# A two-block transformer step on one core: the mixer's input projections ahead of its gates, the state space scan in chunks of eight steps, the gates between the steps of the recurrence

## The chip, the cores and the metric

The kernel is one program on one core of a Trainium2 chip. TensorE (PE) multiplies, VectorE (DVE) and ScalarE (ACT) do the elementwise work, GpSimd (POOL) and SyncE (SP) issue the transfers; they meet only at semaphores. The metric is the device time of one execution in microseconds (us), less is better.

## The reference, cut to what matters

The input is one sequence of 512 tokens of 1024 values. The first block projects it once and mixes four branches of 256 values; each branch is weighted by a sigmoid gate of its own, and the sum goes through `w_o`. A feed forward net and a second block (two attention layers) follow, which the change leaves alone.

```python
mod = (c_act @ ada_w[l] + ada_b[l])[:, None, :]          # 6 x 1024 values: shifts, scales, gates
sh1, sc1, gt1, sh2, sc2, gt2 = jnp.split(mod, 6, axis=-1)
h = rms_norm(x, norm_mix_g[l]) * (1.0 + sc1) + sh1
p = h @ w_in[l]
y_a, v_first = rwkv7_mixer(p[..., :OFF_B], ...)          # a recurrence over 4 heads of 64 x 64
y_b = spatial_gating_mixer(p[..., OFF_B:OFF_C], ...)
y_c = short_conv_mixer(p[..., OFF_C:OFF_D], ...)
y_d = s5_mixer(p[..., OFF_D:OFF_G], ...)                 # 16 groups of 16 channels, 64 complex states each
gates = jax.nn.sigmoid(p[..., OFF_G:]).reshape(bsz, seq, N_BRANCH, D_MODEL)
merged = (gates[:, :, 0] * y_a + gates[:, :, 1] * y_b
          + gates[:, :, 2] * y_c + gates[:, :, 3] * y_d)
x = x + gt1 * (merged @ w_o[l])
h = rms_norm(x, norm_ffn_g[l]) * (1.0 + sc2) + sh2
x = x + gt2 * (jnp.square(jax.nn.relu(h @ ffn_w1[l])) @ ffn_w2[l])

# s5_mixer: x_t = a x_(t-1) + B u_t (complex, diagonal a), y = Re(C x) + d u
_, _, x_re, x_im = lax.associative_scan(_complex_affine_combine, (ar, ai, bu_re, bu_im), axis=1)
y = (jnp.einsum('gcn,bsgn->bsgc', c_re, x_re) - jnp.einsum('gcn,bsgn->bsgc', c_im, x_im))
h = jax.nn.gelu(y) @ glu_w
return h[..., :D_MODEL] * jax.nn.sigmoid(h[..., D_MODEL:])
```

## The kernel before, in words

**Pieces and tiles.** Activations lie transposed, 128 channels on the partitions and 512 tokens along a row. All large weights come as one stream of pieces of 128x1024 (512 KB) in the order in which PE uses them, into a ring of four slots. GpSimd fetches each piece twice: as it is (`load_high`, L330), and, after it has written its negative (L335), added to that (`load_low`, L338), which leaves the rounding rest. So every product of fp32 values is three fast matmuls (high by high, high by rest, rest by high; L1290), and a piece is 24 matmuls over 512 tokens. `project(n, owner)` multiplies n pieces by the eight tiles of `h`, one output tile of a PSUM bank for a piece; `branch_out` multiplies a piece by the two tiles of a branch's result, four output tiles for a piece. There are four such banks (`ps[0]` to `ps[3]`): a product waits until the tile four before it was read by its `owner`. The other four banks (`PA` to `PD`) serve everything else. Every engine runs its own list in program order; `need(name)` waits for the next count of a semaphore. `tile()` waits for the next finished tile, `skip(n)` passes over n tiles that another engine reads.

**Start.** `modulate` (DVE, L448 and L450) multiplies each piece of `ada_w` (48 of them, 512 KB, eight for each of six groups of 1024 outputs) by a value of `c_act` and adds it up; `modulation(group)` on PE (L1314) then sums over the partitions with eight matmuls of one column, fp32, each recorded twice. Groups 0 and 1 are done before `norm` (L412, L414, L366, L367: scale, shift, high part, rest) writes `h`.

**Mixer.** PE takes 12 pieces for the convolution, the spatial gating and s5, does the small matmuls of the spatial gating, and then works through gates and branch outputs beside the s5 scan: `BESIDE` says how many gate pieces and which `branch_out` stand after each of its eight steps. On DVE the scan builds tables of cosines and sines over 512 steps (L887 to L897), then for each of eight tiles of states rotates, scans twice and rotates back (L904 to L920). Seven pieces for `rwkv` follow, s5's gates and outputs, the small matmuls that build the 32-step blocks of the recurrence (`blocks`, L1517), an inversion of triangular blocks on DVE (L555, L556) that is turned around through DRAM by eight transfers (L287), and the recurrence: 16 steps on PE (L1541 to L1560), each with four round trips to DVE and ACT (`rec_y`, `rec_sa`, `rec_state`, `state_set`). At its end stand the last gates, rwkv's output, the modulation's third group (eight more pieces through DVE), the merging of the branches (L841, L848, L366, L367), `w_o` with the fourth and fifth group beside it, the norm, and the feed forward net. The mixer and `w_o` take 61 + 8 pieces.

**ACT** computes the gates' sigmoids (`gate()`, L1091) into a place given by `gate_room(p)`; DVE's `gated(f)` multiplies a branch's tile by it.

Of the kernel before, what the change touches and what calls it, by code (L numbers as in the profile page):

```python
# [28 lines left out]
C = 32  # L29
# [8 lines left out]
S5T = 8  # L38

# [25 lines left out]
BESIDE = [(2, None), (2, 0), (2, None), (2, 1), (1, None), (1, None), (1, None), (1, 1)]  # L65
# [53 lines left out]
def build(nc, A, out):  # L119
# [6 lines left out]
    with ExitStack() as ctx:  # L126
# [24 lines left out]
        arena = sb("arena", [P, ARENA])  # L151
        eye_r = sb("eye_r", [P, P], F32R)
# [7 lines left out]
        t_dram = nc.dram_tensor("pair_inverse", (2, H_A, NCK, C // 2, C), F32, kind="Internal").ap()  # L160

# [26 lines left out]

        def gate_room(p):

            at = (ARENA - 4 * T, ARENA - 4 * T, ARENA - 5 * T, 2048 if p < 28 else 4096)[p // 8] + p % 4 * T
            return arena[:, at:at + T]

        merged, product, glu = x, work[:, 0, :], work[:, 1, :]
        ada_m = place([("sum", (2, D)), ("ada", (ADA, D))], at=ARENA - (ADA + 2) * D)
        conv_m = place([("bg", (2, T)), ("cg", (2, T)), ("z", (2, T)), ("y", (2, T))])
        sg_m = place([("z", (4, T)), ("mu", (T,)), ("d", (2, T)), ("sq", (2, T)), ("std", (T,)), ("rstd", (T,)),
                      ("vn", (2, T)), ("vt", (2, 4, P)), ("ws", (4, P)), ("wsm", (4, P)), ("bs", (2, P)),
                      ("mix", (2, T)), ("caus", (P,))], at=4096)
        s5_m = place([("ct", (8, T)), ("st", (8, T)), ("w", (6, T)), ("bt", (2, 8, P)), ("bpad", (2, 8, P)),  # L200
                      ("bb", (2, 8, 16)), ("b_in", (2, 8, 16)), ("m8", (8, 8)), ("c_in", (2, 2, P)), ("u", (2, T))])
        s5_m["cc"] = s5_m["bpad"]
        assert s5_m["end"] <= ARENA - 4 * T
# [9 lines left out]
                       at=max(rw_in["end"], rw_bd["end"]))  # L213
# [34 lines left out]
        def _(sp):  # L248
# [3 lines left out]
            for q in range(ADA):  # L252
                sp.dma_start(ada[:, q, :], A["ada"][q]).then_inc(S(f"ada_in{q}"), 16)
# [733 lines left out]
        def _(act):  # L987
# [114 lines left out]
            for k in range(4):  # L1102
                gate()
# [656 lines left out]
```

## Time and profile before

| | |
|---|---|
| runs | 2538.32, 2542.22, 2545.75 us, median 2542.22 |
| profiled execution | 2537.91 us, span of the core 2536.1 us |
| busy | PE 2212.2, DVE 1420.2, POOL 845.3, ACT 441.1 us |
| mean granted clock of PE | 0.922 |

The span is the time from the first to the last instruction. "Busy" is the time in which an engine had an instruction under way. The granted clock is the share of 2.4 GHz that PE's clock gate let through: 0.5 is 1.2 GHz, 1.0 is 2.4 GHz.

### The profile page before, as it was taken

The numbers are of one execution on the slowest core, as the hardware profiler recorded it, in microseconds if no ns is written. First come the engines' busy times: TensorE is split into PE (matmuls) and PEld (weight loads), VectorE is DVE, ScalarE is ACT, GpSimd is POOL, SyncE is SP. The second block draws the span as 40 slices with busy tenths as digits, with TensorE's granted clock in tenths as the row PEclk, the third lists the DMA queues.
The fourth block names the chain that finished last, engine by engine and source line by source line (L and its number), as shares of the span: only waits on it lengthen the run. The fifth ranks groups of instructions, "written<-read, shape, count | busy, mean of one in ns | idle before, by whom it ended". The sixth has DMA issues, their size and how long they took to land.

```text
span 2536.1 us, 26355 instructions
## 1 busy us (share of the span) xinstructions
PE 2212.2 (87%) x10172; PEld 1736.6 (68%) x10172; DVE 1420.2 (56%) x1964; ACT 441.1 (17%) x871; POOL 845.3 (33%) x1009
## 2 busy tenths in 40 slices
PE   1967999668787999999988999999898679999995
PEld 1745667557665888887854787878677338878784
DVE  6459775763567344256545572736563665727364
ACT  1010002101000000021056220201210562202021
POOL 1312333110232444444410444444433004444442
PEclk9978999875797999999987999999999789999998
DMA  7635667530695999998820898989877108989895
GB/s 252 135 65 108 141 136 164 96 80 1 174 298 152 205 193 196 191 193 179 183 61 1 193 193 181 195 177 196 194 163 174 31 1 187 193 179 194 182 194 125
DMA packets 115269, 390.31 MB, mean 154 GB/s; under 512 B 20516, under 2 KB 21412, under 8 KB 114632
## 3 DMA queue, kind: packets, MB, share of 16 engines
q0 software_dynamic: 96624, 350.46, 64.8%
q1 hardware_dynamic: 18520, 38.16, 4.3%
q8 instruction: 81, 1.33, 0.2%
q14 instruction: 44, 0.36, 0.0%
HBM read 385.88 MB, written 2.62 MB: 153 GB/s over the span
## 4 chain that ended last, share of the span: by engine, by line
PE 72%; DVE 17%; DMA 5%; ACT 3%; issue 2%; POOL 0%; SPq 0%; DVEq 0%; ACTq 0%
PE ps L1290 61%; DMA arena<-in_ada 3%; PE ps L1379 2%; PE ps L1360 2%; PE ps L1395 1%; DMA w_lo<-in_w 1%; DVE small L706 1%; DVE arena L450 1%; ACT arena L1231 1%; PE ps L1517 1%; ACT arena L1239 1%; DVE work L555 1%; DVE h_lo L367 1%; DVE arena L733 1%; PE ps L1476 1%
## 5 line engine op out<-in xcount | busy, mean ns | idle before, releaser
L1290 PE MATMUL ps<-h_hi,w_hi 128*128 128x512 f32 x1760 | 713.6, 405 | 39.0 <-DVE h_lo L367 27.9
L1290 PE MATMUL ps<-h_lo,w_hi 128*128 128x512 f32 x1760 | 695.7, 395 | 0.0
L1290 PE MATMUL ps<-h_hi,w_lo 128*128 128x512 f32 x1760 | 694.6, 395 | 0.0
L330 POOL DMA_DIRECT2D w_hi<-in_w x334 | 185.7, 556 | 1516.0 <-PE ps L1290 1515.2
L1290 PEld LDWEIGHTS ps<-h_hi,w_hi 128*128 128x128 f32 x1760 | 336.7, 191 | 132.6 <-DVE h_lo L367 28.3
L1290 PE MATMUL ps<-g_hi,w_hi 128*128 128x512 f32 (+1 forms) x880 | 345.6, 393 | 52.0 <-DVE g_lo L367 21.7
L1290 PEld LDWEIGHTS ps<-h_lo,w_hi 128*128 128x128 f32 x1760 | 337.2, 192 | 74.2 <-issue 6.9
L1290 PEld LDWEIGHTS ps<-h_hi,w_lo 128*128 128x128 f32 x1760 | 336.9, 191 | 71.8
L335 POOL TENSOR_SCALAR w_lo<-w_hi 128x1024 fp32r<-128x1024 f32 x334 | 358.6, 1074 | 35.9 <-DMA w_hi<-in_w 30.1
L1290 PE MATMUL ps<-g_lo,w_hi 128*128 128x512 f32 (+1 forms) x880 | 341.6, 388 | 0.0
L1290 PE MATMUL ps<-g_hi,w_lo 128*128 128x512 f32 (+1 forms) x880 | 341.1, 388 | 0.0
L338 POOL DMA_DIRECT2D w_lo<-in_w x334 | 300.4, 899 | 106.0 <-POOL w_lo L335 106.0
L1290 PEld LDWEIGHTS ps<-g_hi,w_hi 128*128 128x128 f32 x880 | 169.4, 192 | 97.0 <-DVE g_lo L367 24.3
L1290 PEld LDWEIGHTS ps<-g_hi,w_lo 128*128 128x128 f32 x880 | 169.6, 193 | 33.3
L1290 PEld LDWEIGHTS ps<-g_lo,w_hi 128*128 128x128 f32 x880 | 169.5, 193 | 32.6 <-issue 0.7
L1256 ACT ACTIVATE arena<-arena,vec 128x512 f32<-128x512 f32 x88 | 71.8, 816 | 412.2 <-DVE arena L728 404.7
L739 DVE TENSOR_TENSOR x<-ps,x 128x512 f32<-128x512 f32 x48 | 33.2, 692 | 183.9 <-PE ps L1290 183.9
L733 DVE SCALAR_TENSOR_TENSOR arena<-arena,vec 128x511 f32<-128x511 f32 x88 | 113.9, 1294 | 3.6 <-ACT arena L1256 0.6
L728 DVE TENSOR_TENSOR arena<-ps,work 128x512 f32<-128x512 f32 x88 | 60.9, 692 | 91.9 <-PE ps L1290 90.5
L960 DVE TENSOR_TENSOR arena<-arena 128x512 f32<-128x512 f32 x32 | 50.3, 1570 | 77.7 <-ACT arena L1178 77.7
L966 DVE SCALAR_TENSOR_TENSOR x<-ps,mod,x 128x512 f32<-128x512 f32 x32 | 24.0, 751 | 111.6 <-PE ps L1290 111.5
L366 DVE CAST g_hi<-arena 128x512 fp32r<-128x512 f32 (+1 forms) x100 | 80.6, 806 | 6.3 <-ACT arena L1112 2.9
(343 smaller groups left out, 2126.7 us busy)
## 6 DMA issues: line engine op xcount, KB each, us to landing
w_hi<-in_w POOLq DMA_DIRECT2D x334, 512.0 KB, 3.9
w_lo<-in_w POOLq DMA_DIRECT2D x334, 512.0 KB, 5.6
arena<-in_ada SPq DMA_DIRECT2D x48, 512.0 KB, 8.8
x<-in_xT SPq DMA_DIRECT2D x1, 2048.0 KB, 17.3
x<-in_xT SPq DMA_DIRECT2D x4, 512.0 KB, 4.7
arena<-in_memT SPq DMA_DIRECT2D x2, 1024.0 KB, 5.4
out_y<-arena SPq DMA_DIRECT2D x1, 2048.0 KB, 6.3
work<-in_mask_dil SPq DMA_DIRECT2D x1, 640.0 KB, 5.9
```

The costliest lines, as they stand in the source:

```text
L330: pool.dma_start(w_hi[:, q % SLOTS, :], A["w"][q]).then_inc(S(f"high_in{q % SLOTS}"), 16)
L335: pool.tensor_scalar(w_lo[:, q % SLOTS, :], w_hi[:, q % SLOTS, :].bitcast(F32), -1.0, 0.0, ALU.mult, ALU.add).then_inc(S("negated"), 1)
L338: pool.dma_start(w_lo[:, q % SLOTS, :], A["w"][q], accum_op=ALU.add).then_inc(S(f"low_in{q % SLOTS}"), 16)
L366: do(dve.tensor_copy(hi, src))
L728: do(dve.tensor_tensor(cv_m["z"][:, side, :], tile()[:], rstd, ALU.mult), "conv_scaled")
L733: do(dve.scalar_tensor_tensor(dst[:, 1:], z[:, :T - 1], w(1), dst[:, 1:], ALU.mult, ALU.add))
L739: update = lambda k: do(dve.tensor_tensor(x[:, k, :], tile()[:], x[:, k, :], ALU.add), "x_done")
L960: do(dve.tensor_tensor(s, r, r, ALU.mult), "relu_used")
L1256: do(act.activation(c[:, j % 2, :], cv_m["z"][:, side, :], ACT.Identity, scale=V("cw2", at), bias=V("cb2", 44 * layer + 22 * side + j0 + j ...
L1290: mm = pe.matmul(bank, w[:, slot, cols], a(k), start=(k == 0 and i == 0), stop=(k == blocks - 1 and i == 2))
L1360: mm = pe.matmul(bank(g)[:, 0:width], at_m["q"][half(g), pair, P * qb:P * qb + P], keys, start=True, stop=not fox)
L1379: mm = pe.matmul(ps[6 + pair % 2][64 * g:64 * g + 64, q0:T], values, pt[pair % 2][:, g, b, q0:T], start=(b == 0), stop=(b == blocks - 1))
```

## The change

The mixer is put into another order and two of its parts are computed in another way; what is computed stays.

- The modulation's groups 0, 1 and 2 leave DVE: `modulation_piece` multiplies each piece of `ada_w` on PE by a single column of `c_act` and adds in PSUM, eight fp32 matmuls of one column for a piece. `modulate` stays for groups 3 to 5. GpSimd's first fetch of weights waits for eight of these pieces.
- s5 works in chunks of Q = 8 steps: the outputs inside a chunk come from a Toeplitz matrix (`toep`), the chunks' states from one scan over 64 chunks for all eight tiles at once. Its tables (`f`, `g`, the kernels) are computed on DVE at the start and by 16 transposes and 32 small matmuls on PE; the kernels, the inputs `u` and the outputs `y` are turned around through DRAM by 8, 16 and 16 transfers.
- Order of the pieces: all 19 input projections first, with the small matmuls of the spatial gating between them, then gates and outputs. Four gate pieces stand between the `blocks`, eight beside the inversion, and 13 pieces are cut into 52 parts of six matmuls, of which three stand in each step of the recurrence (`beside`, `product_steps`). DVE and ACT take their share of that work (`gate_steps`, `step_beside`) in set turns.
- Both norms of the first block write the high part on ACT (`high_shifted`).
- The clearing of the recurrence's padded blocks goes from DVE to ACT (`clear`), between gates.

```diff
-    order = [("conv_in", 6), ("sg_in", 4), ("s5_in", 2)]
-    for branch in ("conv", "sg"):
-        order += [(branch + "_gate", 4), (branch + "_out", 1)] * 2
-    order += [("rwkv_in", 7)] + [("s5_gate", 4), ("s5_out", 2)] * 2
-    return order + [("rwkv_gate", 4), ("rwkv_gate", 4), ("rwkv_out", 1), ("rwkv_out", 1)]
+    order = [("conv_in", 6), ("sg_in", 4), ("s5_in", 2), ("rwkv_in", 7)]
+    order += [("conv_gate", 4), ("conv_out", 1)] * 2
+    order += [("sg_gate", 4), ("sg_out", 1), ("sg_gate", 4), ("s5_gate", 4), ("sg_out", 1)]
+    order += [("s5_gate", 1), ("s5_out", 1)] * 4
+    return order + [("rwkv_gate", 8), ("rwkv_out", 2)]
...
+            pool.wait_ge(S("ada_taken"), 8)
             for q in range(ahead):
                 load_high(q)
...
+            def modulation_piece(q, slots):
+                pe.wait_ge(S(f"ada_in{q % ADA}"), 16 * (q // ADA + 1))
+                for k in range(8):
+                    col = q // 8 * 8 + k
+                    mm = pe.matmul(PA[:, col:col + 1], slots[:, q % ADA, P * k:P * k + P], small[:, 0, q % 8:q % 8 + 1],
+                                   start=(q % 8 == 0 and k == 0), stop=(q % 8 == 7 and k == 7), skip_group_check=True)
+                mm.then_inc(S("ada_taken"), 1)
...
+            for q in range(12):
+                modulation_piece(q, ada_first)
+            pe.wait_ge(S("s5_f"), 1)
+            for i in range(4):
+                for s in range(4):
+                    mm = pe.transpose(ps[i][:, P * s:P * s + P], m["f"][:, i // 2, 4 * (i % 2) + s, :], K("ident"))
...
+            for q in range(12, 16):
+                modulation_piece(q, ada_first)
             total_squares(work[:, 2, :])
-            modulation(0)
-            modulation(1)
+            pe.wait_ge(S("s5_e"), 4)
             project(10, ["dve_freed"] * 6 + ["act_freed"] * 4, ready=h_tile)
...
+                for k in range(KT):
+                    do(dve.scalar_tensor_tensor(work[:, 4 + k % 2, :], x[:, k, :], gain(k), work[:, 3, :], ALU.mult, ALU.mult), "norm_scaled")
+                    if k:
+                        low(k - 1)
+                low(KT - 1)
...
+            for r in range(Q):
+                for k in range(2):
+                    sp.dma_start(s5_m["u_turned"][16 * r:16 * r + 16, 8 * k:8 * k + 8, :],
+                                 u_dram[:, :, k, Q - 1 - r, :].rearrange("g p n -> p g n")).then_inc(S("s5_u_in"), 16)
...
             blocks(pad("a"), pad("b"), 64, 8)
+            project(1, "gate")
             blocks(pad("k"), pad("a"), 64, 8)
+            project(1, "gate")
...
             blocks(pad("b"), lambda p, c: K("ident"), P, 4)
+            branch_out(1, 4)
             project(4, "gate")
+            project(4, "gate")
+            def beside():
+                y = lambda b: (lambda k: g_hi[:, 2 * b + k, :], lambda k: g_lo[:, 2 * b + k, :])
+                slot = open_piece()
+                for i in range(4):
+                    yield from product_steps(slot, 2, *y(1), "gated", first_block=2 * i, first=(i == 0))
+                for _ in range(4):
+                    yield from product_steps(open_piece(), 8, *h, "gate")
+                    slot = open_piece()
+                    for i in range(4):
+                        yield from product_steps(slot, 2, *y(2), "glu_gate" if i % 2 else "gated", first_block=2 * i, first=(i == 0))
+                for _ in range(4):
+                    yield from product_steps(open_piece(), 8, *h, "gate")
...
             for c in range(NCK):
...
+                next(steps, None)
                 if c:
                     need("rec_o_copied", 2)
                 for p in range(2):
                     need("rec_y_copied1" if p else "rec_y_copied")
                     pe.matmul(ps[6 + p][rows[p], 0:HD], bd["tT"][rows[p], c, :], chain_y[rows[p], 0, :],
                               start=True, stop=True).then_inc(S("rec_sa"), 1)
+                next(steps, None)
...
-            project(3, "gate")
+                next(steps, None)
+            for _ in steps:
+                pass
+            project(4, "gate")
             pe.wait_ge(S("o_padded"), 2)
...
-            project(1, "gate")
             pe.wait_ge(S("rw_out"), 2)
-            for half in range(2):
-                branch_out(3, 4)
-            modulation(2)
+            branch_out(3, 8)
+            for q in range(16, 24):
+                modulation_piece(q, ada_m["ada"])
             project(7, "x_done", ready=lambda k: need("merged"))
```

The instructions of PE at the start of the program, before; the names are tiles (`work`: the sum of squares, `arena`: the modulation's sums, `con`: a column of ones), and a row is a kind of instruction with its count.

```order
L1322 MATMUL ps<-work,con 128x512 [waits square_used,con_in]
L1314 MATMUL ps<-con,arena 128x1 [waits ada_sum]
L1314 MATMUL ps<-con,arena 128x1 x7
L1314 MATMUL ps<-con,arena 128x1 [waits ada_sum]
L1314 MATMUL ps<-con,arena 128x1 x7
L1290 MATMUL ps<-h_hi,w_hi 128x512 [waits h_ready,low_in0]
```

The same place of the changed kernel, from the twelfth piece of the modulation on:

```order
L1501 MATMUL ps<-small,arena 128x1 [waits ada_in3]
L1501 MATMUL ps<-small,arena 128x1 x7
L1597 MATMUL ps<-con,arena 128x128 [waits s5_f]
L1597 MATMUL ps<-con,arena 128x128 x15
L1602 MATMUL ps<-arena 128x16 x32
L1501 MATMUL ps<-small,arena 128x1 [waits ada_in0]
L1501 MATMUL ps<-small,arena 128x1 x7
...
L1509 MATMUL ps<-work,con 128x512 [waits square_used]
L1460 MATMUL ps<-h_hi,w_hi 128x512 [waits h_ready,low_in0,s5_e]
```

Where 16 matmuls of one column stood behind the sum of squares, 128 of them (16 pieces), 16 transposes and 32 small matmuls now stand ahead of it.

A step of the recurrence on PE before (`work` holds state and copies, `arena` the blocks):

```order
L1541 MATMUL ps<-arena 64x64 x2
L1545 MATMUL ps<-work,arena 64x64 [waits state_set] x2
L1550 MATMUL ps<-work,arena 64x64 [waits rec_y_copied,rec_o_copied]
L1550 MATMUL ps<-work,arena 64x64 [waits rec_y_copied1]
L1553 MATMUL ps<-arena 128x64 x2
L1556 MATMUL ps<-work,arena 128x64 [waits rec_sa_copied]
L1556 MATMUL ps<-work,arena 128x64 [waits rec_sa_copied1]
```

and in the changed kernel, at the start of its second step:

```order
L1759 MATMUL ps<-arena 64x64 [waits state_set]
L1760 MATMUL ps<-work,arena 64x64
L1759 MATMUL ps<-arena 64x64 [waits state_set]
L1760 MATMUL ps<-work,arena 64x64
L1460 MATMUL ps<-g_hi,w_hi 128x512 [waits gate]
...
L1460 MATMUL ps<-g_hi,w_lo 128x512
L1766 MATMUL ps<-work,arena 64x64 [waits rec_y_copied,rec_o_copied]
L1766 MATMUL ps<-work,arena 64x64 [waits rec_y_copied1]
L1460 MATMUL ps<-h_hi,w_hi 128x512 [waits gated,low_in3]
...
L1460 MATMUL ps<-h_hi,w_lo 128x512
L1770 MATMUL ps<-arena 128x64
```

Six matmuls of a branch output or a gate now stand between the two places at which PE waits for the copies of DVE and ACT, six more ahead of the state's update, and six behind the step.

## Rows read from the trace of the kernel before

**Rows 1.** Windows of the span: length, busy time and instructions by engine, granted clock, DMA.
```profile
core 0: us, PE busy (x) PEld busy (x) DVE busy (x) ACT busy (x) POOL busy (x), PEclk, DMA share, GB/s
0.00:60.20 60.20, 8.83 (x34) 7.65 (x34) 36.45 (x63) 11.90 (x18) 10.02 (x17) 1.00 0.78 266
...
140.20:365.00 224.80, 177.23 (x652) 127.12 (x652) 186.77 (x287) 20.14 (x30) 56.24 (x66) 0.85 0.48 102
365.00:489.70 124.70, 103.95 (x438) 81.97 (x436) 75.82 (x88) 24.93 (x36) 43.27 (x52) 0.92 0.71 150
489.70:557.10 67.40, 42.45 (x544) 37.92 (x544) 48.46 (x92) 3.68 (x5) 10.03 (x12) 0.83 0.44 87
557.10:633.00 75.90, 67.89 (x512) 53.95 (x512) 23.65 (x94) 13.50 (x62) 0.00 (x0) 0.50 0.00 1
633.00:793.60 160.60, 119.25 (x472) 91.60 (x471) 103.29 (x131) 12.64 (x19) 38.22 (x45) 0.78 0.70 203
```

**Rows 2.** Timeline, ACT reads a gate's tile: start, length, wait before it.
```profile
205.17 0.60 ACT L1091 ACTIVATE arena<-ps 128x512 f32<-128x512 f32 x1 [4.84 <-PE ps L1290]
```

**Rows 3.** Timeline of PE: the modulation's sums, at the start and in the feed forward net.
```profile
41.93 3.41 PE L1314 MATMUL ps<-con,arena 128*128 128x1 f32 x16
845.80 1.84 PE L1314 MATMUL ps<-con,arena 128*128 128x1 f32 x16
```

**Rows 4.** Timeline of PE: four transposes, loads for two matmuls, rwkv's last small matmuls.
```profile
153.91 1.11 PE L1421 MATMUL ps<-con,arena 128*128 128x128 f32 x4 [6.88 <-DVE arena L825]
558.82 0.50 PEld L1553 LDWEIGHTS ps<-arena 64*128 64x128 f32 x4
654.80 7.26 PE L1568 MATMUL ps<-con,arena 64*128 64x32 f32 x39
```

**Rows 5.** Two windows of the stretch in which L1568 runs, columns as in rows 1.
```profile
652.00:656.00 4.00, 4.00 (x38) 4.00 (x37) 0.00 (x0) 0.60 (x1) 0.00 (x0) 0.91 0.53 102
656.00:660.00 4.00, 4.00 (x22) 4.00 (x20) 2.50 (x4) 0.00 (x0) 0.00 (x0) 0.50 0.02 4
```

**Rows 6.** Timeline: the norms' last tiles, and the second one's chain from its sum on.
```profile
76.91 0.69 DVE L367 TENSOR_TENSOR h_lo<-work,h_hi 128x512 fp32r<-128x512 f32 x1
764.69 2.06 PE L1322 MATMUL ps<-work,con 128*128 128x512 f32 x2
772.30 0.75 DVE L412 SCALAR_TENSOR_TENSOR work<-x,small,work 128x512 f32<-128x512 f32 x1
792.92 0.69 DVE L367 TENSOR_TENSOR h_lo<-work,h_hi 128x512 fp32r<-128x512 f32 x1
```

**Rows 7.** Timeline of DVE: the s5 tables' first and eighth round, one tile's start, the next's.
```profile
179.13 0.17 DVE L887 TENSOR_TENSOR arena<-arena,small 128x8 f32<-128x8 f32 x1
205.57 1.23 DVE L887 TENSOR_TENSOR arena<-arena,small 128x1024 f32<-128x1024 f32 x1
234.30 0.69 DVE L904 TENSOR_TENSOR arena<-ps,arena 128x512 f32<-128x512 f32 x1
245.53 0.69 DVE L904 TENSOR_TENSOR arena<-ps,arena 128x512 f32<-128x512 f32 x1
```

**Rows 8.** Timeline: PE's blocks, DVE's inversion, its transfer through DRAM, the recurrence's first matmuls.
```profile
489.77 9.98 PE L1517 MATMUL ps<-arena 128*64 128x64 f32 x256 [18.52 <-DVE arena L521]
516.81 1.39 DVE L555 TENSOR_TENSOR work<-arena 128x32 f32<-128x32 f32 x1
549.53 0.34 SPq L280 DMA_DIRECT2D pair_inverse<-arena  x1
557.11 0.48 PE L1541 MATMUL ps<-arena 64*64 64x64 f32 x4 [19.34 <-DMA arena<-pair_inverse]
```

**Rows 9.** Timeline of DVE behind the recurrence: rwkv's output, merging's first and last operation.
```profile
662.17 0.69 DVE L596 TENSOR_TENSOR arena<-arena,ps 128x512 f32<-128x512 f32 x1 [3.42 <-PE ps L1568]
687.25 0.69 DVE L841 TENSOR_TENSOR work<-ps,arena 128x512 f32<-128x512 f32 x1
708.19 0.69 DVE L367 TENSOR_TENSOR h_lo<-x,h_hi 128x512 fp32r<-128x512 f32 x1
```

More of the change, by code:

```diff
@@ L548, in vector_recurrence @@
                 bd_copy(rw_bt, per=4)
+                skip(4)
+                for f in range(4):
+                    gated(f)
                 dve.wait_ge(S("a_in"), 16 * 9)
@@ L1100, in glu_gate, with clear @@
                 count[1] += 1
-            for k in range(4):
-                gate()
-            skip(4)
-            for gates, branch in BESIDE:
-                for k in range(gates):
-                    gate()
-                if branch is not None:
-                    skip(4)
-            for k in range(2):
-                need("s5_sum")
-                do(act.activation(m["w"][:, 2 + k, :], m["w"][:, k, :], ACT.Gelu_apprx_tanh), "s5_gelu")
+            def clear(i):
+                do(act.activation(rw_pad["all"][:, 2048 * i:2048 * i + 2048], K("ident")[:, 0:1].broadcast_to((P, 2048)), ACT.Copy, scale=0.0),
+                   "rw_cleared")
             v = rw_in
@@ L1292, in product @@
                             mm.then_inc(S("w_used"), 1)
+                    if k % 2 and k < blocks - 1:
+                        yield
                 mm.then_inc(S("tile"), 1)
@@ L1447, in _ @@
[L1447 to L1454 removed]
+                    for g in range(2):
+                        mm = pe.matmul(ps[4 + part][halves[g], NQ * s:NQ * s + NQ], m["e"][:, part, s, halves[g]], m["u_turned"][:, 2 * s + g, :],
+                                       start=True, stop=True)
@@ L1459, in branch_out @@
                     for i in range(4):
-                        product(slot, 2, *y, "glu_gate" if glu_tiles and i % 2 else "gated", first_block=2 * i, first=(i == 0))
-            inputs(0)
-            project(4, "gate")
+                        product(slot, 2, *y, "gated", first_block=2 * i, first=(i == 0))
+            v, bd = rw_in, rw_bd
+            project(2, "gate")
+            pe.wait_ge(S("lora_in"), 16)
+            pe.wait_ge(S("rw_m"), 2)
+            pe.wait_ge(S("s5_out"), 2)
@@ new lines, in adapted @@
+            def adapted(rows, first_bank, after=None):
+                for k in range(2):
+                    if after is not None:
+                        pe.wait_ge(S(after), k + 1)
+                    pe.matmul(ps[first_bank + k][:], lora[rows, P * k:P * k + P], v["m"][rows, :],
+                              start=True, stop=True).then_inc(S("rw_adapted"), 1)
+            adapted(slice(0, 32), 4)
+            adapted(slice(32, 64), 6)
+            project(2, "gate")
+            adapted(slice(64, 128), 4, "rw_decay")
@@ L1464, in _ @@
             pe.wait_ge(S("conv_y"), 2)
             branch_out(0, 4)
-            for s, (gates, branch) in enumerate(BESIDE):
-                project(gates, "gate")
-                if s < S5T - 1:
-                    need("s5_bu_used")
-                    inputs(s + 1)
-                if branch is not None:
-                    pe.wait_ge(S("sg_y" if branch else "conv_y"), 2)
-                    branch_out(branch, 4)
-                need("s5_states")
-                for part in range(2):
-                    mm = pe.matmul(ps[6 + s // 4][:], m["cc"][:, part, s, :], m["w"][:, 4 + part, :],
-                                   start=(s % 4 == 0 and part == 0), stop=(s % 4 == 3 and part == 1))
-                mm.then_inc(S("s5_read"), 1)
```

626 lines of the change are left out of this document (380 added, 246 removed).

## The prediction

> **What bounds the kernel now.** I read the windows first [rows 1]. From 140 to 490 us PE is busy for 281 of 349.5 us and DVE for 263: neither engine is full, they wait for each other in turns. From 489.7 to 557.1 PE builds blocks and then stands still until the inverted blocks come back through DRAM. From 557.1 to 633 the recurrence runs alone: 16 steps in 75.9 us, 4.74 each, at a granted clock of 0.50 and with DVE busy for a third of it. In the tail to 793.6 us PE works 119 of 160.6 us. Behind the second norm (its last tile ends at 793.6 [rows 6]) 1742.5 us follow that the change doesn't touch. So the sum has to find only where that last tile ends afterwards. The profiled execution took 2537.91 us (2536.1 of span and 1.8 outside it), 4.3 under the median of 2542.22; I sum in its own time and add 4.3 at the end.
>
> The unit of the sum is a piece of weights. Where only gates stand in line, ACT reads a tile every 0.60 + 4.84 = 5.44 us [rows 2]: 24 matmuls, 0.227 us each.
>
> **Start, to the last tile of the first norm (before: 77.6 us [rows 6]).** Sixteen pieces of modulation come off DVE and become 128 matmuls of one column, each recorded twice. The nearest row has the same form: 8 such matmuls take 3.41 us at the start, 1.84 after a long run of products [rows 3]. I take 3.41, since PE does nothing but such small work here. DMA brought 266 GB/s in these 60 us [rows 1], about 2 us for a piece of 512 KB, so PE and no longer DVE or DMA sets the pace. First piece done at about 7.5 us (my estimate), twelve more 40.9, 16 transposes 4.4 (1.11 for four), 32 small matmuls of two records at 0.125 are 7.8 [rows 4], the last three and the sum's own start counted as four pieces, 13.6: 74.2 us. Then the sum of squares and the root as in the second norm, 7.6 (764.69 to 772.30 [rows 6]): 81.8. The new norm leaves DVE two operations a tile, 16 of 0.75 with a little between them, 12.8 us, where the norm of before took 21.3 (772.30 to 793.61). Together 94.6, **17.0 us later** than before. The s5 tables, now at the start on DVE, are hidden by the 74 us of PE. With 1.84 a piece this stage would end 25 us sooner; that is the gain's bound. The Trainium skill ("TensorE: Matmul & The Clock Gate", section "What's actually happening") says that the throttled state is the default and activity releases it; by it sustained small matmuls might get 1.84. The row speaks against it: with PE busy for 4.00 of 4.00 us at L1568 the granted clock fell from 0.91 to 0.50 [rows 5].
>
> **To the first block (before 77.6 to 489.8, 412.2 us with 51 pieces).** Now 29 pieces stand there. 28 of them at 5.44 are 152.3, the first starts with 1.8 of its own. The small matmuls (the spatial gating, the transposes, the adapted inputs and the head sums of rwkv, s5's inputs 3.4 and its 48 outputs 8) I put at 25.8, by 0.125 to 0.28 us for a record or transpose [rows 4]. Waits at 26.3: 16.6 for the padded inputs of the blocks (18.52 before [rows 8], less the clearing that ACT takes), 4.9 where squares wait for DVE's tables, 2.5 at a root, 1.6 for s5's states, 0.7 for a cold start. What goes is the scan: its tables by doubling (from 179.1 to 205.6 and on) and eight tiles of 11.2 us each (234.30 to 245.53) [rows 7], which is why PE waited. Its replacement is one scan of 64 chunks for all tiles; the turns of `u` and `y` through DRAM lie beside the rwkv and gate pieces, with about 8.5 and 9 us to spare. Eight transfers with the first write took 7.6 us (549.53 to 557.11 [rows 8]), so sixteen take under 15.2 and fit. Sum 206.4: the blocks start at **301**. Of the 189 us, 22 x 5.44 = 120 are pieces only moved behind this point; 69 are waits gone, plus the loss of the start.
>
> **Blocks and inversion (before 489.8 to 557.1, 67.4 us).** The blocks' matmuls and waits were some 26.4 us (to 516.8 on DVE [rows 8]); four gates between them add 21.8, and 2.8 of clearing go: 45.4. DVE then inverts (516.81 to 549.53, 32.8 us) and the transfer takes 7.6, with 5.44 + 1.6 ahead of it for a piece and reads queued in front: 47.4. PE puts a branch output and eight gates beside that, nine pieces, 49.0. The two are about equal, so PE sets the end: with 1 to 2 us for late weights the recurrence starts at **396.5**.
>
> **Recurrence (before 75.9).** In each step stand 18 product matmuls, 18 x 0.227 = 4.08 us, and its 32 small records. Those took 67.9 of 75.9 us over 16 steps, 4.2 us a step, at clock 0.50 [rows 1]; the products hold the clock near 1, so I take half, 2.1, and 0.2 for changes between the forms. 6.4 us a step, 102.4 in all: it ends at **499**. The round trips to DVE and ACT (4.74 - 4.2 = 0.5 us of wait a step before) are covered by parts of six matmuls, 1.36 us, if DVE and ACT come to the copies in time. Uncovered, or with the small ones at 4.2, a step costs up to 8.5.
>
> **Tail (before 160.6).** With R the end of the recurrence: four parts 5.4 and four gates 21.8 with 1.4 between, the last small matmuls of rwkv 10 (L1568: 7.26 for 39 records [rows 4]): R + 38.6. rwkv's output and the merge: the latter took 21.6 us (687.25 to 708.88) behind the modulation's third group, which held DVE for most of the time from 662 to 687 [rows 9]; that group is now on PE, eight pieces behind `branch_out`, R + 55 to R + 77.6 (three at 1.84, five at 3.41). The merge ends at R + 66 and waits for nobody. `w_o`: 8 x 5.44 + 2.5 = 46, R + 123.6, with its DMA about equal (203 GB/s over this stretch before [rows 1]). Last addition and square 7.9, root 7.6, norm 12.8: **R + 152**, 8.7 us less than before.
>
> Sum: 499 + 152 = 651 in place of 793.6, -142.6 (+17.0 start, -205.8 to the blocks, +28.1 blocks and inversion, +26.5 recurrence, -8.6 tail; gates moved, not gone, are in these). 2537.9 - 142.6 = 2395.3, and 4.3 to the median: **2399 us**. By busy time the figure is plausible: before, PE was idle for (349.5 - 281.2) + (67.4 - 42.5) + (160.6 - 119.3) + 51 at the start + 8 = 193 us of the first 794 us, and its products are as many as before.
>
> **The rivals.**
> *Forecast, 0.56.* 2399, with its own range 2385 to 2415: an unknown of 10 us each in the small matmuls and the waits of the second stage.
> *The small matmuls run at the fast clock, 0.16.* Start 16 x 1.57 = -25 and five pieces in the tail -8: 2366. For it: PE has no gaps in that stretch. Against it: [rows 5].
> *The steps of the recurrence are longer, 0.18.* DVE and ACT now serve gates in set turns between the copies. If each step waits 1.5 us more, +24: 2423; if the clock stays at 0.50 there, a step costs 4.2 + 18 x 0.43 = 11.7, +85: 2484. For it: each turn misplaced stops PE with everything behind it. Against it: products at 0.227 us held the clock at 0.92 in the stretch before [rows 1], and DVE was busy for only 23.65 of 75.9 us.
> *The turns through DRAM are late, 0.06.* They consist of runs of 256 bytes, 32 transfers. If each is 1 us slower than the pair inverse's share of 7.6 us, some 20 us are lost beyond the slack: 2420. The Trainium skill ("DMA: Bandwidth & Descriptors", section "Specifications") wants at least 512 bytes for the full rate; no row of this kernel has the shorter form. The pieces of weights also share the queues at up to 203 GB/s [rows 1].
> *The other side, 0.03: the interleaving fails.* If a product part waits for a tile that DVE frees only after its copy, nothing overlaps, and at clock 0.50 a step takes 11.7 + three round trips of 1.2 = 15.3 us. That is the point from which it decides: 142.6 / 16 = 8.9 over 6.4. Then it is 2540 or above. A DVE that was two thirds idle speaks against it. That the order has no effect at all (0.01) would need PE's 193 idle us to come back elsewhere.
>
> **Range and chances.** 2360 takes in the fast clock, 2450 the longer steps and late turns up to half their price; outside are the slow clock of the recurrence and the other side. Three runs here spread by 7 us, 0.3%, about what tells a change from none. Faster 0.96, same 0.01, slower 0.03.
>
> **What would show it.** Eight matmuls of a modulation piece in 3.41 us each at the start, and the last tile of the first norm near 95; the first block near 301; the first matmul of the recurrence near 397, 6.4 us a step at a granted clock near 1 and no wait above 0.5 us in it; the end near 499; the last tile of the second norm near 651; 1742.5 us behind it as before. Wrong would be: pieces of 1.84 at the start, waits for `rec_y_copied` or `gated` inside the steps, a wait for the turned `u` or `y`, or the inversion's transfer ending after the gates beside it.

## The result and the profile after

The changed kernel takes 2457.72 us (median of 4 runs, 2453.9 to 2476.27) beside 2542.33 of the kernel before: a ratio of 0.968 with a 95% interval of 0.963 to 0.973. That is 85 us less where 143 were forecast, and 8 us outside the stated range of 2360 to 2450. The profiled execution took 2453.9 us with a span of 2452.1.

First the windows of the changed kernel's trace, cut where its stages end (columns as in [rows 1]); the last two are the tail and all that lies behind the second norm.

```profile
core 0: us, PE busy (x) PEld busy (x) DVE busy (x) ACT busy (x) POOL busy (x), PEclk, DMA share, GB/s
0.00:94.60 94.60, 75.29 (x359) 69.72 (x359) 48.15 (x110) 20.67 (x32) 10.04 (x17) 1.00 0.61 182
94.60:320.50 225.90, 199.14 (x905) 158.14 (x903) 125.58 (x219) 44.17 (x51) 70.72 (x84) 0.90 0.67 141
320.50:420.20 99.70, 90.80 (x761) 76.34 (x761) 54.84 (x98) 8.48 (x13) 32.72 (x39) 0.96 0.79 154
420.20:550.00 129.80, 129.80 (x803) 92.34 (x804) 47.17 (x127) 22.71 (x79) 30.18 (x36) 0.98 0.48 99
550.00:708.30 158.30, 138.43 (x606) 114.03 (x604) 89.93 (x105) 18.97 (x27) 43.53 (x48) 0.81 0.76 212
708.30:2452.10 1743.80, 1614.90 (x7236) 1278.21 (x7235) 915.70 (x1164) 351.97 (x696) 661.53 (x785) 0.96 0.76 162
```

Against the forecast, stage by stage:

| stage | forecast | measured | off |
|---|---|---|---|
| start, to the first norm's last tile | 94.6 | 94.7 | +0.1 |
| to the first block | 206.4 | 225.8 | +19.4 |
| blocks and inversion | 95.5 | 99.7 | +4.2 |
| recurrence (420.2 to 548.1) | 102.4 | 127.9 | +25.5 |
| tail (548.1 to 708.3) | 152 | 160.2 | +8.2 |
| the rest | 1742.5 | 1743.8 | +1.3 |

The clock column's 1.00 can't be taken at its word in the first window, here or in [rows 1]. PE's timeline has there

```profile
85.11 0.63 PE L1460 MATMUL ps<-h_lo,w_hi 128*128 128x512 f32 x1
85.54 0.63 PE L1460 MATMUL ps<-h_hi,w_lo 128*128 128x512 f32 x1
```

These products start 0.43 us apart, as others do in this trace at a granted clock of 0.50; from 89.5 us on it is 0.23. So for the start I go by the lengths of rows.

In the recurrence PE is busy for every one of the 129.8 us at a clock of 0.98: no turn of DVE or ACT is late. So its length is PE's own work. Here is the fifth step on PE's timeline (start, length of a row; left out are products, L1770 with L1772, and the end of the second half):

```profile
454.55 0.32 PE L1759 MATMUL ps<-arena 64*64 64x64 f32 x2
454.81 0.33 PE L1760 MATMUL ps<-work,arena 128*64 128x64 f32 x2
455.06 0.33 PE L1759 MATMUL ps<-arena 64*64 64x64 f32 x2
455.32 0.33 PE L1760 MATMUL ps<-work,arena 128*64 128x64 f32 x2
455.58 0.50 PE L1460 MATMUL ps<-h_hi,w_hi 128*128 128x512 f32 x1
...
457.17 0.33 PE L1766 MATMUL ps<-work,arena 64*64 64x64 f32 x4
...
459.63 0.33 PE L1774 MATMUL ps<-work,arena 128*64 128x64 f32 x2
459.89 0.32 PE L1775 MATMUL ps<-work,arena 64*64 64x64 f32 x2
460.05 0.28 PE L1776 MATMUL ps<-arena 64*64 64x64 f32 x2
460.26 0.33 PE L1774 MATMUL ps<-work,arena 128*64 128x64 f32 x2
...
462.47 0.32 PE L1759 MATMUL ps<-arena 64*64 64x64 f32 x2
```

A step is 462.47 - 454.55 = 7.92 us, and 14 of the 15 distances between steps are that within 0.02. A part of six products takes 457.17 - 455.58 = 1.59 us and not 6 x 0.227 = 1.36. The 32 small records take the other 3.15 us: 1.03 for L1759 and L1760, 0.26 for L1766, 0.60 for L1770 and L1772, 1.26 for L1774 to L1776 of both halves. One detail turned out to matter most: four records of L1766 take 0.26 us (457.17 to 457.43, where the next product begins), as long as two of L1759.

s5's outputs, which I had put at 8 us, take 24.3 (205.12 to 229.4); PE's timeline at their start:

```profile
205.12 0.41 PE L1655 MATMUL ps<-arena 128*128 128x64 f32 x2 [2.32 <-DVE arena L1030]
205.46 0.66 PE L1658 MATMUL ps<-arena 64*128 64x63 f32 x4
...
209.44 0.69 PE L1655 MATMUL ps<-arena 128*128 128x64 f32 x2
210.06 1.11 PE L1658 MATMUL ps<-arena 64*128 64x63 f32 x4
```

and the windows of the two parts of that stretch:

```profile
205.10:208.00 2.90, 2.88 (x19) 2.50 (x19) 2.79 (x4) 0.00 (x0) 0.00 (x0) 1.00 0.00 0
208.00:229.40 21.40, 21.40 (x80) 18.35 (x79) 0.12 (x1) 0.00 (x0) 0.00 (x0) 0.50 0.00 0
```

It is 96 records, six for each of 16 groups. The clock falls to 0.50 at 208 us while PE is busy without a gap, as it did at L1568 before [rows 5].

The inversion's result comes back late (SyncE's timeline: write, eight transfers; then the first matmul of the recurrence on PE):

```profile
408.01 0.34 SPq L320 DMA_DIRECT2D pair_inverse<-arena  x1
411.86 4.57 SPq L327 DMA_DIRECT2D arena<-pair_inverse  x8
...
420.19 0.47 PE L1759 MATMUL ps<-arena 64*64 64x64 f32 x2 [6.19 <-DMA arena<-pair_inverse]
```

12.2 us in place of 7.6 [rows 8], and PE stood for 6.2 of them. At the start four pieces of the modulation take 13.7 us, and the sum of squares (L1509) begins at 73.96 against a forecast of 74.2.

### The profile page after: what moved, and what is told of

Read it like the earlier page. It is cut to its first block, busy times and chain, and to the rows that moved or that the text cites. A ratio compares the mean times of both kernels' runs of the same rounds, so it can differ in the third digit from the quotient of the medians.

```text
span 2452.1 us, 27262 instructions
## 1 busy us (share of the span) xinstructions
PE 2248.4 (92%) x10664; PEld 1788.8 (73%) x10664; DVE 1281.4 (52%) x1822; ACT 467.0 (19%) x897; POOL 848.7 (35%) x1009
## 4 chain that ended last, share of the span: by engine, by line
PE 79%; DVE 12%; DMA 4%; ACT 3%; issue 2%; POOL 0%; SPq 0%; DVEq 0%; ACTq 0%
PE ps L1460 64%; PE ps L1501 3%; DMA w_lo<-in_w 2%; PE ps L1566 2%; PE ps L1547 2%; PE ps L1582 2%; DVE small L787 1%; DVE work L612 1%; PE ps L1714 1%; ACT arena L1400 1%; DMA w_hi<-in_w 1%; ACT arena L1408 1%; DVE arena L814 1%; PE ps L1658 1%; DVE arena L613 1%
## 5 line engine op out<-in xcount | busy, mean ns | idle before, releaser
L1460 PE MATMUL ps<-h_hi,w_hi 128*128 128x512 f32 x1760 | 706.0, 401 | 28.0 <-DVE h_lo L456 19.8
L1501 PE MATMUL ps<-small,arena 128*128 128x1 f32 x384 | 79.1, 343 | 8.8 <-DMA arena<-in_ada 8.8
L1501 PEld LDWEIGHTS ps<-small,arena 128*128 128x128 f32 x384 | 79.0, 321 | 8.9 <-issue 8.8
```

Source lines behind the costliest of these rows:

```text
L1460: mm = pe.matmul(bank, w[:, slot, cols], a(k), start=(k == 0 and i == 0), stop=(k == blocks - 1 and i == 2))
L1501: mm = pe.matmul(PA[:, col:col + 1], slots[:, q % ADA, P * k:P * k + P], small[:, 0, q % 8:q % 8 + 1], start=(q % 8 == 0 and k == 0), stop ...
```

## The experiments

Times are medians of 4 runs each; the changed kernel's median of 2457.7 is from a set of runs of its own, the experiments share runs of the kernel before in groups of four (2542.7, 2545.8 and 2546.2), so that a few us between medians of different sets tell nothing. Where a difference is below 10 us I go by the stretch of the trace that the edit touches. Two profiles of the same code differ by up to 5 us between s5's outputs and the inversion, and their clocks differ there: from L1655 to the inversion's first operation it is 168.3 us at a mean clock of 0.88 in the changed kernel's profile and 173.5 at 0.85 in that of the third experiment, which is the same up to there.

### 1. Products ahead of the recurrence

```diff
-            steps = beside()
+            for _ in beside():
+                pass
             pe.wait_ge(S("tT_in"), 16 * 8)
...
-                next(steps, None)
```

The last line stands three times in a step; the set turns of DVE and ACT go with it.

> The 52 parts of products run before the recurrence (beside the wait for the inverted blocks) and not in its steps; the recurrence stands alone again. My theory: the steps of the changed kernel take 7.92 us because TensorE itself is full (4.77 us for three parts with their changes of form, 3.15 us for 32 small records), nothing waits for DVE or ACT. Then the products take 13 x 5.44 = 70.7 us from 414 on, the recurrence again 16 x 4.74 = 75.9 us at a granted clock of 0.50, and its last step ends near 561 in place of 553.7 (with the last four parts): about 7 us slower than the changed kernel, own time near 2461 us. Rival, that the set turns of DVE and ACT or their traffic lengthen the steps: without them 10 us or more faster, below 2445.

Measured: 2481.7 us, ratio 0.976 (0.973 to 0.979), 24 us above the changed kernel and not 7. The products were done in time and the recurrence began at 486.3, as the sum had it. But it took 90.6 us and not 75.9. The window, and a piece of PE's timeline:

```profile
486.30:576.90 90.60, 83.14 (x514) 65.53 (x514) 23.64 (x94) 14.11 (x63) 0.00 (x0) 0.51 0.03 5
```
```profile
514.03 0.47 PE L1762 MATMUL ps<-work,arena 128*64 128x64 f32 x2
514.44 0.47 PE L1761 MATMUL ps<-arena 64*64 64x64 f32 x2
...
515.78 0.48 PE L1767 MATMUL ps<-work,arena 64*64 64x64 f32 x4 [0.47 <-DVE work L641]
```

Two records of L1762 take 0.41 us (514.03 to 514.44), four of L1767 the same. The rival (turns of DVE and ACT lengthen the steps) is out, since the steps without them are no cheaper. My sum of a step fell too: the same number of records at the same clock cost 15 us more than in [rows 1]. What differs is their order. The kernel before issues both halves' first matmul (heads on partitions 0 to 63, then 64 to 127), then both halves' second; the changed one issues a half's first and second, then the other half's. This is in the rows of the change, in the section ahead of the prediction: L1541 x2 and L1545 x2 against L1759, L1760, L1759, L1760. The last three matmuls of a step stand one half after the other in both kernels (PE's timeline before; L1559 and L1560 of the first half left out):

```profile
559.93 0.47 PE L1558 MATMUL ps<-work,arena 128*64 128x64 f32 x2
...
560.95 0.47 PE L1558 MATMUL ps<-work,arena 128*64 128x64 f32 x2
```

### 2. The order of before, products still ahead

```diff
-                for p in range(2):
-                    need("state_set", 1 if c or p == 0 else 0)
+                need("state_set", 2 if c else 1)
+                for p in range(2):
                     pe.matmul(ps[4 + p][rows[p], 0:HD], bd["akT"][rows[p], c, :], ...)
+                for p in range(2):
                     pe.matmul(ps[4 + p][rows[p], 0:HD], pad("a")(p, c), state[:, now, p, :], ...)
```

and likewise for the state's two matmuls.

> As the kernel with the products ahead of the recurrence, but its small matmuls in the order of the kernel before (both halves' first matmul, then both halves' second). Theory of the halves: its steps go from 5.66 back to 4.74 to 4.9 us, 12 to 14 us less than that kernel (own time 2484.6, to about 2472), so of the 24 us by which that kernel is slower than the changed one 12 to 14 are the order. Rival, that its slow steps come from the place (another granted clock, banks 4 and 5 in place of 0 and 1): steps of 5.66 stay.

Measured: 2466.2 us, 15.5 less than the first experiment; the recurrence takes 73.4 us in this window:

```profile
488.70:562.10 73.40, 65.37 (x514) 51.77 (x513) 23.64 (x94) 14.10 (x63) 0.00 (x0) 0.54 0.04 7
```

The banks are those of the changed kernel, so of the 17 us between 90.6 and 73.4 the order makes 15.5: at 0.50 a step takes 4.73 us in place of 5.70. In the rest the clock has a part, which fell some 4 us later here (mean 0.54 against 0.51).

### 3. The halves side by side in the interleaved steps

The same edit in the changed kernel, and the last three matmuls of a step in pairs as well.

> The small matmuls of a step are issued so that the two of a pair (heads of partitions 0 to 63, then 64 to 127) stand next to each other in each of its three groups, in place of one half's matmuls and then the other's. Theory, from the first kernel with the products ahead (90.5 us for a recurrence that took 75.9 in the kernel before, with the same matmuls in another order): neighbours on different halves of the array overlap, neighbours on the same half do not. Then the 8 records of the first group take about 0.62 in place of 1.03 us and the 12 of the last about 0.8 in place of 1.26: 0.85 us a step, 13.6 in all; own time near 2440. Rival, that a record of this size costs its 0.1 us in any order at the fast clock (loading of weights): no difference, 2454.

Measured: 2441.8 us, ratio 0.959 (0.956 to 0.963), 16 us under the changed kernel. A step from its first small matmul to the next step's:

```profile
441.13 0.33 PE L1759 MATMUL ps<-arena 64*64 64x64 f32 x4
441.39 0.34 PE L1761 MATMUL ps<-work,arena 128*64 128x64 f32 x4
...
445.69 0.34 PE L1776 MATMUL ps<-work,arena 128*64 128x64 f32 x4
445.95 0.33 PE L1778 MATMUL ps<-work,arena 64*64 64x64 f32 x4
446.12 0.28 PE L1780 MATMUL ps<-arena 64*64 64x64 f32 x4
...
447.93 0.33 PE L1759 MATMUL ps<-arena 64*64 64x64 f32 x4
```

6.80 us, 1.12 less. Of these, 0.51 come from the first group (441.13 to 441.65, 0.52 in place of 1.03), which has the order of the kernel before again, and 0.62 from the last three (0.64 in place of 1.26), which that kernel did not have in pairs. The small records take 6.80 - 3 x 1.59 = 2.03 us. That this is close to the 2.1 of the prediction is chance: in the order of the kernel before they would take about 0.52 + 0.26 + 0.59 + 1.26 = 2.63 at this clock, an estimate from the rows of these two profiles. The rival, a fixed cost of a record, is out.

### 4. The halves in two other places

```diff
-                for g in range(2):
-                    (toep of g; both parts of g)
+                (toep of both g); for part in range(2): for g in range(2): ...
...
-            for p in range(2):
-                for c in range(NCK):
+            for c in range(NCK):
+                for p in range(2):
                     mm = pe.matmul(ps[4 + p][:, C * c:C * c + C], opad[rows, c, :], K("sum32")[rows, :], ...)
```

> The rule of the halves tried in two other places of the changed kernel: in s5's outputs the four records of one group that use partitions 0 to 63 of the weights stand next to those that use 64 to 127 (before, one group's and then the other's), and in rwkv's last 32 small matmuls the halves alternate. Theory: a neighbour on the other half of the rows overlaps. The four records then take 0.52 us in place of 1.04 (16 such sets, 8 us), the last matmuls 5.2 in place of 10.4 us: 13 us less, own time near 2441. Rival, that only matmuls of 64 columns in different column halves overlap and rows don't: s5's outputs keep their 24.3 us, and at most 5 us are gained.

Measured: 2450.4 us (2444.0 to 2456.8). In the stretches themselves the theory holds: s5's outputs take 15.4 us (202.54 to 217.96) in place of 24.3, the last matmuls 4.49 in place of 10.40. Of PE's timeline at a clock of 0.50, then at the last matmuls and behind them:

```profile
205.33 1.11 PE L1655 MATMUL ps<-arena 128*128 128x64 f32 x4
206.37 1.12 PE L1659 MATMUL ps<-arena 64*128 64x63 f32 x8
...
566.61 4.49 PE L1788 MATMUL ps<-con,arena 64*128 64x32 f32 x64
576.49 0.80 PE L1460 MATMUL ps<-g_hi,w_hi 128*128 128x512 f32 x1 [5.39 <-DVE g_lo L410]
```

Eight records of L1659 in the time of four before. In L1788 the order counts at the fast clock too: 37 records fit into its first 2.0 us at 1.00, where the changed kernel has 28 in 3.0 us at 0.98. Its gain is half given back: PE waits 5.39 us for DVE's output in place of 2.76. In place, 8.9 + 5.9 - 2.6 = 12 us are gained; the median shows 7, and its four runs spread by 13.

Neighbours on different halves write to different banks of PSUM here, which would be another cause. The bank alone doesn't do it: L1655 fills all partitions and columns, its two matmuls now stand next to each other on two banks, and four of its records still take 1.04 us (205.33 to 206.37), against 1.24 before. And for halves of the columns no second bank is needed. The blocks alternate them within one bank, and in the changed kernel, at a clock of 1.00, 64 records take 2 us:

```profile
329.80 2.09 PE L1714 MATMUL ps<-arena 128*64 128x64 f32 x64
```

For halves of the partitions no run has both in one bank.

### 5. s5's outputs between products

```diff
+            parts = two_pieces()
             for s in range(S5T):
+                if s:
+                    next(parts)
...
-            project(2, "dve_freed")
```

`two_pieces` are the two projections that stood behind; each `next` issues six of their matmuls.

> The 96 small records of s5's outputs (24.3 us, granted clock fallen to 0.50 after 3 us of them) stand in eight groups of 12 with a part of six product matmuls between them. Theory, that the clock made them long: 0.145 us a record as in the first three groups, 13.9 us and seven changes of form of 0.23, so the stretch is 8 to 9 us shorter and the blocks start near 312 in place of 320.5; own time near 2445. Rival, that the records are long by their own work (128 columns of weights each) whatever the clock: no gain, the changes of form cost 1.6 us more, blocks near 322.

Measured: 2452.9 us. In place, outputs and seven parts take 206.1 to 238.6, 32.4 us, where the changed kernel needs 24.3 + 7 x 1.36 = 33.8: 1.4 gained, not 8. But the clock fell 0.5 us into the outputs, ahead of the first part, and came back at 223; before and behind that, PE's timeline has

```profile
219.76 1.11 PE L1666 MATMUL ps<-arena 64*128 64x63 f32 x4
...
223.86 0.65 PE L1666 MATMUL ps<-arena 64*128 64x63 f32 x4
```

So the clock does set a record's length (1.04 to 0.59 us from start to start of what follows), and the forecast gain failed because 17 of the 32 us ran at 0.50. From 226 to 240 us the same mixture ran at 1.00; whether it holds the clock once it is up everywhere, or what brought it back at 223, this run doesn't tell. Both my theory's gain and the rival's loss are wrong. The median is 5 us under the changed kernel's, too little to tell the two apart.

### 6. The modulation of the tail between rwkv's outputs

```diff
-            branch_out(3, 8)
-            for q in range(16, 24):
-                modulation_piece(q, ada_m["ada"])
+            for i in range(8):
+                product(slot, 2, *y3, "gated", first_block=2 * (i % 4), first=(i % 4 == 0))
+                modulation_piece(16 + i, ada_m["ada"])
```

> In the tail each of the eight modulation pieces stands behind one tile of rwkv's branch output (six products) in place of all eight behind the eight tiles. Theory, that their 3.0 us a piece is the low clock: 1.84 us a piece and 1.59 a tile, 27.4 us for both in place of 37.7, the last tile of the second norm 8 to 10 us earlier (near 699), own time near 2445. Rival, that w_o behind it is bound by its weight transfers (waits of 0.5 to 1.4 us are there now): the pieces get short, but the norm ends only 0 to 4 us earlier.

Measured: 2457.4 us, no change. The clock is 0.50 until 608.6 us, with products between the pieces, and 1.00 from 612 on; the pieces get shorter once it is up:

```profile
602.69 3.41 PE L1501 MATMUL ps<-small,arena 128*128 128x1 f32 x16
...
612.15 1.84 PE L1501 MATMUL ps<-small,arena 128*128 128x1 f32 x16
```

Both together take 35.3 us and not 27.4 (37.7 in the changed kernel), and behind them the waits grow: PE's wait for DVE's sums from 3.7 to 5.1 us, those for weights from 3.2 to 3.8. From the branch's first tile to the norm's first product it is 106.1 against 106.6 us. The rival was right: the weights and DVE's part of the modulation bound this stretch.

### 7. Three parts beside the inverse

```diff
             steps = beside()
+            for _ in range(3):
+                next(steps)
             pe.wait_ge(S("tT_in"), 16 * 8)
```

> Three of the parts run ahead of the wait for the inverted blocks. Theory: that wait (6.2 us of idle TensorE) is set by DVE and the transfers alone, and the recurrence by TensorE's own work: the three parts fill 4.1 us of it, the recurrence starts at 420 as before and the parts end 4.8 us earlier; own time near 2449. Rival, that the transfers are slow because weights are fetched beside them, and one more fetch falls there: the recurrence starts 1 to 3 us later and the gain is 2 us or less.

Measured: 2470.5 us, 13 more. Write and transfers took 16.6 us (413.28 to 429.92) in place of 12.2, and with the parts three ahead of DVE's and ACT's set turns PE waits inside the steps; eight of the 15 distances are 7.92 us, the others 9.1 to 12.2. PE's longest waits there:

```profile
PE ps L1761 <- DMA arena<-pair_inverse: 6.6, 1, 6.6
PE ps L1460 <- DVE work L996: 6.3, 6, 1.2
PE ps L1460 <- ACT arena L1233: 4.5, 4, 1.2
```

The rival was right on the transfer; the waits in the steps neither theory had.

### 8. One fetch of weights behind the inverse

```diff
+                if q + ahead == 44:
+                    pool.wait_ge(S("tT_in"), 16 * 8)
```

> One fetch of weights (the one that GpSimd issues at 409 us) waits until the inverted blocks are back. Theory: the write and the eight transfers took 12.2 us (408.0 to 420.2) in place of the 7.6 of the kernel before because weights move beside them; without that fetch they take 8 to 9, the recurrence starts at 416 to 417, and the piece is in time (it is wanted near 445): 3 to 4 us faster, own time near 2450. Rival, that the eight issues on SyncE and the writes set it, or that what is in flight already disturbs enough: 420 as before, and the time is the same.

Measured: 2454.3 us (2450.7 to 2463.8), by which alone it can't be told from the changed kernel. Write and transfers took 9.6 us (412.42 to 422.0) in place of 12.2, the issues 3.75 in place of 4.57; nothing waited for the late piece. So 2.6 of the 4.6 us over the 7.6 of before are this one fetch, and the write (3.85 us, as in the changed kernel, 2.0 before) keeps the rest.

### 9. The second group on VectorE again

```diff
-            for q in range(12):
+            for q in range(8):
                 modulation_piece(q, ada_first)
...
+            for q in range(8):
+                do(dve.scalar_tensor_tensor(ada_sum1, ada_slot(q), c_act[:, q:q + 1], ada_sum1, ALU.mult, ALU.add))
...
-            for q in range(12, 16):
-                modulation_piece(q, ada_first)
+            for k in range(8):
+                mm = pe.matmul(PA[:, 8 + k:9 + k], ada_sum1[:, P * k:P * k + P], K("ones")[:, 0:1], start=True, stop=True)
```

DVE's eight pieces have places of their own, and its tables `g` stand ahead of the squares.

> At the start TensorE takes only the first eight pieces of the modulation; the other eight are multiplied and summed on VectorE as in the kernel before, behind its tables, and summed by eight matmuls. Theory: the start is bound by TensorE's 16 pieces of 3.41 us, VectorE idles from 30.6 to 61.8 us. VectorE then ends at about 49, its squares at 55, the sum of squares is made near 55.5 in place of 74.0, all behind it 18 us earlier; own time near 2435. Rival, that the transfers (16 pieces, x, and the first weights, which still wait for eight pieces, 36 us) bound it then: VectorE waits for its pieces, 8 to 12 us gained, near 2444; or that the turn of u is then late for TensorE.

Measured: 2443.3 us, 14 less. PE's timeline of the start:

```profile
9.14 27.52 PE L1522 MATMUL ps<-small,arena 128*128 128x1 f32 x128 [9.14 <-DMA arena<-in_ada]
...
57.16 2.08 PE L1530 MATMUL ps<-work,con 128*128 128x512 f32 x2 [2.86 <-DVE work L431]
```

The sum of squares comes 16.8 us earlier, and so does L1655. At the inversion's first operation the profile is 11.8 us ahead (361.6 against 373.4): 5.0 us are lost in the stretch in which profiles of the same code differ by as much. The start was bound by PE's pieces; now DVE bounds it, for which PE waits 3.6 and 2.9 us.

### 10. Without the wait ahead of the first fetches

```diff
-            pool.wait_ge(S("ada_taken"), 8)
```

> GpSimd's first fetches of weights don't wait for eight pieces of the modulation. Theory: the first 60 us are bound by TensorE's pieces of 3.41 us and not by transfers; only the first pieces come later, since 4 MB of weights move beside them: the first modulation matmul at 10 to 13 us in place of 8.8, the first norm 2 to 4 us later, own time 2456 to 2458. Rival, that the wait shields all the pieces: without it TensorE waits for pieces again and again, 10 us or more are lost; or that it does nothing: 2454.

Measured: 2468.4 us, 11 more. At its place it costs what was expected: the first piece at 10.89, one further wait of 3.15 us, the sum of squares 2.4 us later. The profiled run lies 11 us above the changed kernel's; 2.4 are this, about 3 arise before the inversion, where such profiles differ anyway, and 6 behind the second norm (1749.6 us in place of 1743.8). I can't tie the last two to the edit, and they stay open.

### 11 and 12. Together

The edits of 3, 8 and 9 in one kernel, then those and the edits of 4; their diffs stand above.

> Three edits together: the halves side by side in the recurrence's steps (15.9 us faster by itself), the modulation's second group on VectorE (14.4 us), one fetch behind the inverse (3.5 us). They lie in different stretches, so theory: they add up, 31 to 34 us under the changed kernel, a median near 2425. Rival: what one gives back the next stretch takes (a clock that falls at another moment, weights late): 20 to 25 us, near 2435.

Measured: 2420.8 us, ratio 0.951 (0.948 to 0.955), 37 less than the changed kernel, so they add up.

> The three edits and the halves side by side in s5's outputs and in rwkv's last matmuls: by the theory of the halves 13 us less than without these, near 2412.

Measured: 2412.3 us, ratio 0.947 (0.944 to 0.951): 45 us under the changed kernel, 134 under the one before, and the best of all. The edits of 4 are worth 8.5 us here, where 13 were expected.

## Why the prediction was wrong

- **Direction and mechanism right.** Waits of PE went, gates cover the inversion and the recurrence's round trips. The own time was off by 2453.9 - 2395.3 = 58.6 us.
- **Start: right, in part by luck.** 3.41 us a piece, no fast clock; the loss of 17.0 us came out as summed. But in the sum two errors cancel: the first piece was done at 8.8 + 3.4 = 12.2 and not 7.5 us, while I had counted one piece too many (3.4, for the start of the sum of squares) and 1.7 too much for the transposes and small matmuls. The rival of the fast clock was wrong there, and in the tail worth nothing even where it held (experiment 6).
- **Recurrence: the failed step, 25.5 us.** "The products hold the clock near 1, so I take half, 2.1": the clock was 0.98, yet the small records took 3.15 us, 17 us more in 16 steps. This has two causes of about the same size. First, I carried the 67.9 us of the kernel before over to matmuls in another order, though the two pieces of PE's program stood in my own text: 0.51 us a step at the fast clock, 8 in 16 (experiment 3), and 15.5 in 16 at the slow one (experiments 1 and 2). Second, the fast clock doesn't halve such records: 4.2 us at 0.50 become some 2.6 in the same order and not 2.1, 8 us more. What experiment 3 gained beyond the first cause comes from the last three matmuls, whose order the change had left as it was. A second term was too small: 0.2 us a step for changes between forms of matmul, where three parts cost 3 x (1.59 - 1.36) = 0.69, 8 us in 16. The first step began at the low clock and cost 2.7 more; its last part, 1.6, lies behind the end that I measured to. My own bound for a step, 8.5 with the small ones at 4.2, held. The rival of longer steps had nearly the size (+1.5 us a step), by a mechanism (late turns of DVE and ACT) that did not occur in the changed kernel.
- **s5's outputs, 16.3 of the 19.4 us of the second stage.** 48 matmuls at 8 us was too small: they are 96 records, the first six took 0.92 us at the fast clock (205.12 to 206.04), by which all would have been 14.7, and the clock fell to 0.50 on them. I had used that fall [rows 5] against the fast modulation and not here. Experiment 4 shows that 8.9 us of it are order again. The waits of this stage were 26.8 us in sum (26.3 forecast). The other 3.1 us I did not take apart; a piece behind small matmuls takes 5.66 in place of 5.44 us.
- **Inverse, 4.2 us.** PE's cover was 49.2 us as forecast, but the chain beside it took 43.2 (364.8 to 408.0) + 12.2 in place of 39.8 + 7.6. The 7.6 us had been read where PE stood still and GpSimd issued no fetch (69 GB/s in these 7.6 us, 166 in the 12.2); experiments 7 and 8 show that fetches beside the transfer make it longer.
- **Tail, 8.2 us.** The modulation's pieces took 3.0 in place of 2.8 us each, `w_o` waited 3.2 for weights and 3.7 for DVE's sums. "DMA about equal" was a bound, and both bind by turns.
- **Turns of u and y.** Hidden, as forecast: PE shows no wait for either.
- **Wait of the first fetches.** I costed it at nothing; at the start it saves 2.4 us, and without it the whole kernel took 11 us more (experiment 10), of which the rest stays open.

## What to carry to other kernels

Before a duration of small matmuls is carried to a new place, compare their order: here pairs on different halves of the partitions or columns cost half of pairs on the same half, so let loops over halves be innermost. Don't halve them for a doubled clock; read them at the clock that they will run at. Cost each change between wide products and small matmuls (0.23 us here for a part), and for a transfer read the time in a stretch with the same traffic. Where an engine is handed another's work, see whether it becomes the bound while the other idles, and split it.

## What was not expected of the hardware

- Two small fp32 matmuls that use different halves of the array overlap if they are neighbours. Four records of L1766 (halves alternating) take 0.26 us at the fast clock, as two records of one half do (L1759); at 0.50 it is 0.41 for the one as for the other. With 64 partitions of weights by 128 columns, eight records take 1.05 us alternating and four take 1.04 otherwise. Records that fill all 128x128 gained little: 0.26 us each against 0.31, at 0.50 (experiment 4). The Trainium skill ("TensorE: Matmul & The Clock Gate", section "Architectural detail: the array is 16× 32×32, not 1× 128×128") says that one part of the array can multiply while others still load weights; these traces agree as far as they go.
- The fast clock does not halve such a record: 0.41 against 0.26 us for four, 1.6 times.
- A granted clock of 0.50 came with PE busy for 21.4 of 21.4 us in s5's outputs, and in experiment 5 with products mixed in until 223 us; behind that the same mixture ran at 1.00.
